# Pooling mixer of a four-layer trunk kernel: constant mean tables on the matrix engine, and an earlier issue point for the next layer's first weight panels

## The reference, cut to what matters

```
for gi, win in enumerate((2, 4, 8, 16)):           # 256 features each
    start = clip(t - win // 2, 0, L); end = clip(t + win - win // 2, 0, L)
    mean  = (cs[end] - cs[start]) / (end - start)   # centred window mean over tokens
    out_g = (mean - h) @ w[gi]                      # 256 x 256
```

## Time and profile before

| what | value |
|---|---|
| median of 3 runs | 1528.62 us (1527.22 to 1530.3) |
| the profiled execution's own time | 1528.77 us |
| its span, first to last instruction | 1527.0 us |
| PE busy | 1423.2 us, 93% of the span |
| DVE / ACT / POOL busy | 766.3 / 327.3 / 88.4 us |
| moved by DMA | 436.84 MB, mean 286 GB/s |

### The profile page before, as it was taken

One profiled execution on the slowest core, in us unless ns is written; L12 is line 12 of the kernel. 1 busy time (PEld: TensorE's weight loads), 2 busy tenths in 40 slices (PEclk: granted clock), 3 DMA queues, 4 the chain that ended last, 5 costly groups with the idle time before them and its releaser, 6 DMA issues. The chain is left out here.

```text
span 1527.0 us, 18085 instructions
## 1 busy us (share of the span) xinstructions
PE 1423.2 (93%) x6557; PEld 735.3 (48%) x6557; DVE 766.3 (50%) x1861; ACT 327.3 (21%) x731; POOL 88.4 (6%) x97
## 2 busy tenths in 40 slices
PE   6998998999789999899999999999998998999975
PEld 3344535444255443556666666454443446454432
DVE  1334205554767544666666666037445464166534
ACT  1105304111242111611111111031112226141101
POOL 0000010000220001000000000010001010100001
PEclk9999999999899999999999999999999999999987
DMA  9979957999896998745555553547998730069995
GB/s 380 409 290 403 413 205 322 392 423 422 336 394 268 420 423 323 275 144 174 175 174 176 174 176 132 230 174 312 422 421 334 289 117 1 28 247 398 422 423 203
DMA packets 125204, 436.84 MB, mean 286 GB/s; under 512 B 7520, under 2 KB 63680, under 8 KB 86848
## 3 DMA queue, kind: packets, MB, share of 16 engines
q1 hardware_dynamic: 109744, 396.93, 66.6%
q10 hardware_dynamic: 11920, 26.24, 4.5%
q0 software_dynamic: 3456, 12.58, 2.3%
HBM read 414.20 MB, written 21.53 MB: 285 GB/s over the span
## 5 line engine op out<-in xcount | busy, mean ns | idle before, releaser
L1031 PE MATMUL bank<-gate_up_weights,hT_gathered 128*64 128x512 f32 (+1 forms) x1280 | 255.7, 600 | 15.4 <-SPq L561 15.4
L864 PE MATMUL bank<-panel,hT 128*128 128x512 f32 x384 | 166.4, 593 | 3.5 <-DMA panel<-in_ret_w_in 2.6
L1031 PEld LDWEIGHTS bank<-gate_up_weights,hT_gathered 128*64 128x64 f32 (+1 forms) x1280 | 81.6, 133 | 181.5 <-issue 181.5
L1045 PE MATMUL bank<-down_weights,actT 128*64 128x512 f32 (+1 forms) x640 | 138.6, 603 | 2.5 <-ACT actT L2237 2.5
L1485 DVE SCALAR_TENSOR_TENSOR ada_sums<-panel,cond_columns,ada_sums 128x384 f32<-128x384 f32 x224 | 121.2, 612 | 0.0
L864 PEld LDWEIGHTS bank<-panel,hT 128*128 128x128 f32 x384 | 72.9, 190 | 91.9 <-issue 87.4
L675 PE MATMUL bank<-panel,hT 128*128 128x512 f32 x240 | 105.7, 598 | 0.9 <-ACT hT L2018 0.9
L675 PE MATMUL bank<-panel,oT 128*128 128x512 f32 x192 | 84.3, 595 | 1.3 <-ACT oT L2141 1.3
L1016 PE MATMUL bank<-h_hi,P 128*128 128x512 f32 x192 | 81.7, 425 | 0.0
L2224 ACT ACTIVATE silu<-bank 128x256 f32<-128x256 f32 x36 | 13.8, 385 | 307.5 <-PE bank L1031 307.5
L1016 PE MATMUL bank<-h_lo,P 128*128 128x512 f32 x192 | 75.7, 394 | 0.0
(11 more groups left out here) (340 smaller groups left out, 1954.8 us busy)
## 6 DMA issues: line engine op xcount, KB each, us to landing
gate_up_weights<-in_gate_up_halves SPq DMA_DIRECT2D x148, 1024.0 KB, 13.5
down_weights<-in_down_rows SPq DMA_DIRECT2D x74, 1024.0 KB, 13.6
panel<-in_ada_panels SPq DMA_DIRECT2D x54, 1024.0 KB
panel<-in_w_ada SPq DMA_DIRECT2D x16, 1536.0 KB
ada_panel_third<-in_ada_panels SPq DMA_DIRECT2D x18, 1024.0 KB
y_by_slot<-y_rows ACTq DMA_DIRECT2D x32, 512.0 KB, 8.0
panel<-in_ret_w_in SPq DMA_DIRECT2D x16, 1024.0 KB
panel<-in_attn_w_qkv SPq DMA_DIRECT2D x5, 2048.0 KB
```

The lines of the kernel that those rows point to most:

```text
L864: last = PE.matmul(ps[t][:], hT[:, k, t * 128:(t + 1) * 128], panel[f % 2][:, k, :], start=k == 0, stop=k == KD - 1)
L1031: last = PE.matmul(ps[2][width * s:width * s + width, :], hg[:, j, k, width * s:width * s + width], gu_ring[w][:, 2 * k // KD, :, k % (KD ...
L1045: last = PE.matmul(ps[6 + half][width * s:width * s + width, :], actT[:, c, width * s:width * s + width], dn_ring[w][:, c, half * 512:half ...
```

## The change

The pooling mixer becomes a product with constant tables. `k_pool` holds for each window a matrix "mean minus identity" between tokens: 128 columns for the prompt, 256 for the first latent tile, and 136 (SPAN) for the second, which reaches 8 tokens back. x scaled, not turned and not modulated, is the stationary operand, so the product comes out turned and pooled at once; DVE and ACT then multiply it by the modulation scale only. The 18 DVE instructions, the padded buffers, three POOL memsets and the 0.8 MB DMA of `k_cnt` go; a 1.06 MB DMA of `k_pool` (`pool_table`) comes, issued on ACT's queue at the end of layer 0. The PE order in the mixer is new, and the pool products of tile 1 wait for `moe_added` 3, because their banks hold the ninth row's sums.

The wait on `quads_done` ahead of the next layer's first panels moves behind them, for all three layer changes.

```diff
             if l:
                 sp.wait_ge(sem("row_gateup"), ROWS * l)
-                sp.wait_ge(sem("quads_done"), l)
                 if l % 3 == 2:
                     for s in (f, f + 1):
...
             if l % 3 == 2:
                 for j in range(2):
                     load_ret_ada(l + 1, j, j)
+                sp.wait_ge(sem("quads_done"), l)
                 sp.wait_ge(sem("unit_sum"), 2 * TILES * (l - 1) + 2)
...
                     load_row(sp, l, 0, 0, 1, tuple((sem("ada_product"), last_late[s]) for s in GU_OF[0]))
+                    sp.wait_ge(sem("quads_done"), l)
                     load_row_down(sp, l, 0, 0, 1)
                 else:
+                    sp.wait_ge(sem("quads_done"), l)
                     sp.wait_ge(sem("unit_sum"), 2 * TILES * (l - 1) + 2)
...
+                    atleast(sp, "o_gateup", done + p + 1)
+                    sp.sem_inc(sem("o_read"), 1)
...
+    POOL_BANKS = (2, 3, 6, 5)
+    def pe_pool_turn(pe, l, t):
+        n = 2 * l
+        xs = x_scaled(n, t)
+        if t == 1:
+            pe.wait_ge(sem("moe_added"), TILES * l)
+        for half, scaled in enumerate(("xs_dve", "xs_act")):
+            pe.wait_ge(sem(scaled), TILES * n + t + 1)
+            for k in range(4 * half, 4 * half + 4):
+                lhs, g = xs[:, k * 128:(k + 1) * 128], k // 2
+                if t == 0:
+                    last = PE.matmul(ps[half][:, k % 4 * 128:k % 4 * 128 + 128], lhs, pool_m[:, g, 0:SEQ], start=True, stop=True)
...
+                elif t == 1:
+                    PE.matmul(ps[POOL_BANKS[g]][:, k % 2 * DEC:k % 2 * DEC + DEC], lhs, pool_m[:, g, SEQ:SEQ + DEC],
+                              start=k % 2 == 0, stop=False)
+                else:
+                    last = PE.matmul(ps[POOL_BANKS[g]][:, k % 2 * DEC + DEC - SPAN:k % 2 * DEC + DEC], lhs, pool_m[:, g, SEQ + DEC:],
+                                     start=False, stop=k % 2 == 1)
...
     def pe_pool(pe, l):
...
+        pe.wait_ge(sem("table_landed"), 16)
+        pe_pool_turn(pe, l, 0)
+        pe_pool_turn(pe, l, 1)
+        pe_static_product(pe, WOVEN)
         pe.wait_ge(sem("mods_ready"), l + 3)
...
+        for i, bank in enumerate((0, 1, 4)):
+            pe_broadcast(bank, 2, i // 2, i % 2).then_inc(sem("gate_ps"), 1)
+        pe_pool_turn(pe, l, 2)
+        pe.wait_ge(sem("gate_bc"), 8 * l + 1)
+        pe_broadcast(0, 2, 1, 1).then_inc(sem("gate_ps"), 1)
+        pe_static_product(pe, WOVEN + 1)
         panel_landed(pe, f)
         for half in range(2):
...
+            else:
+                pe.wait_ge(sem("hT_act"), TILES * (n + 1))
+                for i in range(4):
+                    pe_broadcast((6, 3, 4, 5)[i], 5, i // 2, i % 2).then_inc(sem("gate_ps"), 1)
+                for idx in range(WOVEN + 2, STATIC_ADA):
+                    pe_static_product(pe, idx)
                 pe.wait_ge(sem("gate_bc"), 8 * (l + 1))
-            pe.wait_ge(sem("pool_u"), 2 * half + 2)
...
-                                         uT[:, q, POFF[t]:POFF[t] + 128], panel[f % 2][:, q, 0:256],
+                                         hT[:, q, t * 128:(t + 1) * 128], panel[f % 2][:, q, 0:256],
...
+        pe_static_columns(pe, 5)
         pe_turn(pe, 2 * l + 1, 0)
...
+        def pool_latent(l):
+            n = 2 * l
+            for g in range(2):
+                dve.wait_ge(sem("hT_ps"), 2 * TILES * n + 3 + g)
+                for k in range(2 * g, 2 * g + 2):
+                    last = V.tensor_scalar(hT[:, k, SEQ:T], ps[POOL_BANKS[g]][:, k % 2 * DEC:k % 2 * DEC + DEC], mod_col(1, k, 1), None,
+                                           ALU.mult)
+                last.then_inc(sem("hT_dve"), 1)
...
-                order = "e0 e1 e2" if n == 0 else "s0 t0 s1 x0 x1 e0 s2 x2 e1 e2" if l % 3 == 1 else "s0 x0 e0 s1 x1 s2 x2 e1 e2"
+                order = "e0 e1 e2" if n == 0 else "s0 s1 x0 x1 u0 s2 x2 b0 b1 b2 v2 b3 v3 m0 m1 m2 m3" if l % 3 == 1 else "s0 x0 e0 s1 x1 s2 x2 e1 e2"
             elif l % 3 == 1:
-                order = "a0 a1 a2 s0 s1 s2 x0 x1 e0 x2 e1 p0 e2 p1 p2"
+                order = "a0 a1 a2 c5 s0 s1 s2 x0 x1 e0 x2 e1 p0 e2 p1 p2"
...
             more_quads(e, more, passes, l)
+            if l == 0:
+                e.dma_start(pool_m[:], A["k_pool"]).then_inc(sem("table_landed"), 16)
```

More of the change, by code:

```diff
@@ L193, in build_trunk @@
     (oT, qT), _ = region(("oT", [HEADS, T]), ("qT", [HEADS, T]))
[L195 to L198, removed]
+    (pool_m,), _ = region(("pool_table", [4, SEQ + DEC + SPAN]), start=mix0 + size([NQKV]) + size([TILES, D]))
     (yTo, rMT), dn_end = region(("yT_odd", [RH, T]), ("ret_mask", [RH, 128]), start=dn2_at)
@@ L1217, in mod_col, with hT_out @@
         return mods[:, v * KD + k, c:c + 1]
[L1219 to L1221 removed]
+    def hT_out(k, t):
         return hT[:, k, t * 128:(t + 1) * 128]
@@ L1332, in residual @@
                 evacuate(l, 1, 0)
+                collect(5)
             else:
@@ L1930, in _ @@
                 attention(l)
-            elif l % 3 == 1:
-                pool(l)
-            else:
+            elif l % 3 == 2:
                 retention(l)
-            if l == 1:
-                collect(5)
             residual(l)
@@ L2017, in evacuate @@
             for k in range(lo, hi):
-                last = S.activation(hT_out(l, sub, k, t), ps[2 * t + 1][:, (k - 4) * 128:(k - 3) * 128], ACT.Identity,
+                last = S.activation(hT_out(k, t), ps[2 * t + 1][:, (k - 4) * 128:(k - 3) * 128], ACT.Identity,
                                     bias=mod_col(3 * sub, k, c), scale=mod_col(1 + 3 * sub, k, c))
@@ L2044, in norm @@
                         .then_inc(sem("logit_parts"), 1)
-                elif what == "t":
-                    e.dma_start(icnt[:], A["k_cnt"].rearrange("(o g) w -> o g w", o=1).broadcast_to([128, 4, PW]))\
-                        .then_inc(sem("table_landed"), 16)
+                elif what == "u":
+                    e.wait_ge(sem("hT_ps"), 2 * TILES * n + 2)
+                    for k in range(4, KD):
+                        last = S.activation(hT_out(k, 0), ps[1][:, (k - 4) * 128:(k - 3) * 128], ACT.Copy, scale=mod_col(1, k, 0))
+                    last.then_inc(sem("hT_act"), 1)
+                elif what == "v":
+                    e.wait_ge(sem("hT_ps"), 2 * TILES * n + 3 + t)
+                    for k in range(2 * t, 2 * t + 2):
+                        last = S.activation(hT[:, k, SEQ:T], ps[POOL_BANKS[t]][:, k % 2 * DEC:k % 2 * DEC + DEC], ACT.Copy,
+                                            scale=mod_col(1, k, 1))
+                    last.then_inc(sem("hT_act"), 1)
+                elif what == "b":
+                    gate_half(8 * l + t, gate_bc, t, (0, 1, 4, 0)[t])
+                elif what == "m":
+                    gate_half(8 * l + 4 + t, moe_gate, t, (6, 3, 4, 5)[t])
                 elif what == "a":
@@ L2054, in norm, with gate_half @@
                     square(n, t)
-        def gate(n, banks):
-            into = (gate_bc, moe_gate)[n % 2]
-            for c in range(2):
-                for half in range(2):
-                    e.wait_ge(sem("gate_ps"), 4 * n + 2 * c + half + 1)
-                    S.activation(into[:, c, half * 512:half * 512 + 512], ps[banks[2 * c + half]][:], ACT.Copy)\
-                        .then_inc(sem("gate_bc"), 1)
+        def gate_half(done, into, i, bank):
+            e.wait_ge(sem("gate_ps"), done + 1)
+            S.activation(into[:, i // 2, i % 2 * 512:i % 2 * 512 + 512], ps[bank][:], ACT.Copy).then_inc(sem("gate_bc"), 1)
         def pile_copy():
@@ L2096, in attention @@
                 if h == HEADS and l == 0:
-                    gate(0, (0, 1, 2, 3))
-                    gate(1, (0, 1, 2, 3))
+                    for i in range(8):
+                        gate_half(i, (gate_bc, moe_gate)[i // 4], i % 4, i % 4)
                 e.wait_ge(sem("qkT_ps"), NQK * a + h + 1)
@@ L2281, in _ @@
                 attention(l)
-            elif l % 3 == 1:
-                gate(2 * l, (0, 1, 2, 3))
-                gate(2 * l + 1, (0, 1, 2, 3))
-                stack_copy(5)
-            else:
+            elif l % 3 == 2:
                 retention(l)
@@ L2340, in _ @@
                     G.tensor_tensor(of_keys(64, t), of_keys(32, t), hpow[:, 0:KV], ALU.pow).then_inc(sem("qk_rstd"), 1)
-            elif l % 3 == 1:
-                for lo, hi in ((0, POFF[0]), (POFF[0] + SEQ, POFF[1]), (POFF[1] + DEC, PW)):
-                    last = G.memset(hp[:, :, lo:hi], 0.0)
-                last.then_inc(sem("cleared"), 1)
-            else:
+            elif l % 3 == 2:
                 with pool.Fori(0, RH) as h:
```

84 lines of the change are left out of this document (34 added, 50 removed).

## The result

| | kernel before | changed kernel |
|---|---|---|
| runs side by side | 20 | 20 |
| median | 1529.14 us (1526.1 to 1535.36) | 1534.88 us (1526.93 to 1541.15) |
| standard deviation | 2.3 us | 3.9 us |
| the profiled execution's own time | 1528.77 us | 1527.61 us |
| its span | 1527.0 us | 1525.8 us |

The ratio of the two is **1.0028, with a 95% interval of 1.0016 to 1.004**: slower by 0.28%, about 4.3 us, where I had forecast 1526.9 us, no measurable change, 1525 to 1530 for that case and 1521.2 to 1532.8 for 8 in 10. The median of 1534.88 lies outside both. The runs also lie further apart than before.

A forecast was written before the change was run, and what follows sets the result against it. PE, busy 93% of the span, was taken as the bound, with gains only between expert rows. Mixer -2.9, layer 2 0, layer 3 +1.0: -1.9 on 1528.77 gives 1526.9 us; range 1525 to 1530, for 8 in 10 1521.2 to 1532.8.

The forecast's parts named there:

- The product on PE: Layer 1's mixer: PE's run from tile 1's pool product to the projection's end takes 30.9 us, before 31.3.
- The tail: Mixer's end after the projection: one term and one addition remain, gaining 0.9 us; `collect(5)` on DVE gives back 0.2.
- The first rival: Into layer 1: gathers hardly delayed by early panels, mixer 6.3 us earlier, 1523.0 us in all; chance 0.38.
- Sum 4.3 us for the fourth gather, and 4.4 for the end of the sums of tile 2: Into layer 1: delay of the gathers by early panels and table, bounds 0 and 11 us.
- the burst: Into layer 1, from about 390.8: some 2 us with gathers at 0.07 in place of 0.35, 1.6 us late.
- the third queue: Into layer 1: the 1.06 MB table in 8 KB packets leaves gathers 0.125 MB/us for 4.2 us, 2.7 late.
- about equal turns: DMA queues get the same number of packets, 71 against 64, so packet size sets the gathers' share.
- the sum for the mixer: Layer 1: x complete 2.2 + 0.9 - 0.2 = 2.9 us earlier, with gathers 4.4 late.
- Layer 3: Change into layer 3: PE waits for x, and early panels make the fourth gather 1.0 us later, 0 to 3.
- it lands when it did: Into layer 2: the early panel gets little until the gathers end, so it lands unchanged; net effect taken as 0.
- the gathers stand behind the panels of 8 KB packets: Slower rival, `take` 3 to 5 of layer 0: gathers 10 us late, +5.2 us, 1534; chance 0.18.
- The rule of the Trainium skill: DMA engines serve queues by 9 to 17 descriptors; gathers get a fifth against big panels, giving the slower rival's time.

The follow-up runs named there:

- Tables alone: The changed kernel with the first panels of every layer again issued after `quads_done`, as before the change; ratio 0.9966 to the kernel before.
- the early table: The changed kernel with panels late at all three layer changes and the pool table's DMA issued ahead of the gathers; ratio 0.9957 to the kernel before.
- early panels alone: The kernel before with only the wait on `quads_done` moved, at all three layer changes, and no pool tables; ratio 1.0052.
- large packets first: The changed kernel with products' panels 31 to 33 loaded ahead of the pool weights into layer 1; ratio 1.0032 to the kernel before.
- the second profile: The changed kernel run again without any edit; ratio 1.0011 to the kernel before, median 1531.53 us.
- panels early only there: The changed kernel with the pool table issued ahead of the gathers and panels early into layer 3 only; ratio 0.9961 to the kernel before.
- the two fastest versions: Changed kernel, table issued ahead of the gathers, panels early into layer 2 only: 0.9926; the same with panels into layers 1 and 3 behind the fourth gather: 0.9938.

## Why the prediction was wrong

- **The product on PE: right.** I had 30.9 us for the run; it took 29.3 and 29.8. The terms that I subtracted were there: no wait for a panel, and full clock. The granted clock was 0.68 at 414 to 422 and 1.00 from 422 on, where it had been 0.76 through most of the run. The windows of the changed kernel (busy time of PE, PEld, DVE, ACT, POOL; clock, DMA share, GB/s):

```profile
414.00:422.00 8.00, 7.45 (x31) 6.74 (x32) 4.76 (x11) 3.86 (x9) 0.70 (x2) 0.68 0.53 220
422.00:433.00 11.00, 11.00 (x81) 7.28 (x80) 2.35 (x5) 3.74 (x8) 0.37 (x1) 1.00 0.70 250
433.00:448.00 15.00, 15.00 (x105) 10.07 (x103) 3.17 (x7) 5.43 (x13) 5.93 (x5) 1.00 0.77 292
```

- **The tail: right.** From the end of the projection to the next turn it is 447.63 to 450.48, 2.85 us, before 3.85. The sum had 0.9 less 0.2.
- **With undelayed gathers the whole would be right.** The first rival gave 6.3 us for the mixer. Tables alone gave 5.2 us of time and 5.3 of stage A, with the table still in the gathers' way. With the early table it is 0.43%, 6.6 us, and A is 6.2 to 9.0 below that of the kernel before.
- **The failed step: "Sum 4.3 us for the fourth gather, and 4.4 for the end of the sums of tile 2".** The delay was 11.0 us in the first profile and 5.3 in the second, and 8.2 in the kernel with early panels alone. What I had summed was there: the burst, the third queue, about equal turns. I had treated the queue's rate as one number, and ended the gathers when their bytes were through. The trace shows instead a thin tail of 0.23 MB from 406 to 414 beside large packets. The fourth `take` at 407.76 falls into it. From 410 to 411 q0 has 8 packets, where equal turns on all 16 DMA engines pass some 38 in a us (151 in 4 us with large packets first). An estimate from these two counts is that about three of the 16 engines still had gathers to bring in, each in equal turns with the large packets; the mean rate of the queue says nothing of these last engines. And I priced the fourth gather alone, though the second, stopped first (18.6 us against 12.1), holds DVE's multiplication and PE's scatter behind it. In this profile the scatter ended at 408.18, 0.9 before the end of the fourth `take`, and so cost nothing; with early panels alone it ended at 411.19, 0.7 behind it. With 11 us, the sum for the mixer turns from -2.9 to +3.7, and to +2.1 with the 1.6 by which PE's run was shorter; A grew by 2.2. With the second profile's 5.3 us and its run of 29.0 it is -3.9; A fell by 3.8.
- **Layer 3: later, as forecast; how much of it is time stays open.** I took 1.0, with 0 to 3. The fourth `take` is at 20.2 us on average over eight profiles with early panels into layer 3 and at 17.6 over the six with late ones, 2.6 later. Stage C has a mean of 373.9 against 369.8. That is 4.1, from single profiles, whose scatter is about 2 us each; the pair that differs in this alone shows 3.6 in C but 0.0004 in the ratio, and two of the six late ones also wait for the gathers. Against the kernel before alone nothing is to be seen: its `take` is at 19.6 and the changed kernel's two at 19.5 and 20.6, its C is 372.45 and theirs 370.61 and 374.44. The wait of 3.01 from which I took the size was that of one execution: with the panels as late, tables alone waits 1.34 and the kernel with the early table 1.94. And I had left a term out there, PE's clock. The scatter of the ninth row into layer 3, first with panels early only there, then with none early:

```profile
1168.30 8.32 PE L1135 MATMUL bank<-y_rows,logit_parts 128*128 128x512 f32 x12 [3.30 <-issue]
```

```profile
1166.56 5.42 PE L1134 MATMUL bank<-y_rows,logit_parts 128*128 128x512 f32 x12 [2.94 <-issue]
```

It starts 16.2 and 15.9 us after the ninth row's gate/up, and takes 2.9 us longer for the same 12 records. PE had stood idle for 3.30 us ahead of it in the one and 2.94 in the other; in the 10 us from 1162.06 the granted clock is 0.75, so for a part of them at the 1.2 GHz level, and in those from 1160.68 of the other profile 1.00. The first turn of layer 3 behind it comes 27.0 and 23.7 us after gate/up, and these 3.3 us are most of the 3.6 in C.
- **Layer 2: "it lands when it did" was wrong, and yet the forecast of 0 holds as far as is shown.** The panel landed earlier: PE waits 0.88 or 0.89 for x in all nine profiles with early panels, and 2.50 to 4.08 for the panel in the five with late ones. But x came later by as much, since the gathers are delayed here too (fourth `take` at 18.2 to 20.9 us, against 17.0 to 17.8). The first projection starts 28.1 us after the ninth row's gate/up on average with early panels and 28.0 with late ones. What is left is the clock: in three of the five late profiles its 16 records take 8.83 to 10.20 us in place of 7.1. B has a mean of 567.4 with early panels and 568.3 with late ones, a gain of about 1 us that is no larger than the scatter.

Sum of the mean stages: A with tables and late panels 199.25 (two profiles) and with early ones 204.83 (two of the changed kernel), so -6.4 + 5.6 against before; layer 2 -0.9; layer 3 +4.1. It makes +2.4 us. The measured ratios 1.0028 and 1.0011 are +4.3 and +1.7. So the account closes within its scatter, which is some us, as each mean is of single profiles and the kernel before has one; the two later terms aren't shown by themselves. The result is the rival "the gathers stand behind the panels of 8 KB packets", to which I gave 0.18. That its time, 1534, is so near is in part luck: it had 10 us for the gathers in every execution, where 5.3 and 11.0 were measured, and a loss of 0.5 into layer 2 that no profile shows. Its mechanism is only in part shown. That early panels into layer 1 make the loss is shown by the runs, and that a packet of 8 KB leaves a gather a third of the bytes by the queues with large packets first. That their packet size, and not their amount, is the reason for the lost time isn't.

The rule of the Trainium skill that I weighed ("DMA: Bandwidth & Descriptors", section on queues, rings and completion order) speaks of turns of 9 to 17 descriptors. The counts of the changed kernel, 74 to 75 and 31 to 41 to 40, and those with large packets first, 151 to 147, are about equal turns, and by the estimate above the tail is too. In these stretches it was not by that rule that the slower time came out. The burst, 164 to 28, is no equal turn, and no run here shows what makes it.

Open: why the delay differs from execution to execution of one kernel (5.3 and 11.0 us), and why a few DMA engines hold their gathers so much longer than the rest. The queue's totals suggest that they do, but no row here shows it by engine.

## What to carry to other kernels

Before a load is issued earlier, look at what else is in flight at that moment and who waits for it: a prefetch that nobody was waiting for can stop a small, late-bound transfer that everybody waits for. Price a small transfer by when its last piece lands beside the large ones, and not by its queue's mean rate. Price the first of a series of transfers as well as the last, since an engine that waits in order for one holds all that stands behind it. Ask whether a longer wait of PE costs its clock besides. And when two edits travel together, time them apart: here one gave 0.34% and the other took 0.52%, and the two fastest versions kept the early loads only at the layer change where a panel was the last to arrive, though no profile shows their lead to come from there.

## What the hardware showed that I had not expected

- Two profiles of the same kernel have the fourth gather at 26.6 and at 20.9 us, and yet the two executions took 1527.61 and 1527.55 us: what the first lost in A it won back in B and C. So the gathers alone don't explain how far whole runs lie apart. The standard deviation is 3.9 and 4.1 us in the two sets of the changed kernel, but 3.5 with tables alone, where all panels are late, and 2.2 with large packets first, where all are early; the kernel before has 2.1 to 2.8.
- The stretch ahead of layer 0's ninth row, in which these kernels do the same, lasts from 381.2 us (changed kernel) to 386.5 us (tables, early table). From 20 to 60 us PE is busy for 34.45 us in both, but passes 148 records in the first, at a granted clock of 0.96, and 136 in the second, at 0.83.
- The last 0.23 MB of the gathers needed 8 us (406 to 414) beside 3.15 MB of large packets, where about equal turns a few us earlier had given them 0.27 MB in one (400 to 401).
- A table that is in flight before the gathers begin costs nothing that can be seen (fourth `take` at 15.3 to 15.7 in five profiles, 15.6 before); issued with them it has the fourth `take` at 18.1 and 19.1.
